# Projection of a hybrid encoder layer: four of five column groups by one level of Strassen, gate columns moved to the first group

## The reference, cut to what matters

```python
h = _rmsnorm(x, g_pre) * (1.0 + scale[:, None, :]) + shift[:, None, :]
proj = h @ w_in                       # 4096x1024 by 1024x4616, fp32
(ml_qk, ml_v, ml_o, ml_z, ml_gates,
 sb_q, sb_k, sb_v, sb_z) = jnp.split(proj, IN_SPLITS, axis=-1)
ml_qk = jax.nn.silu(_causal_conv(ml_qk, conv_w, conv_b))
i_pre = ml_gates[..., :ML_HEADS] + b_igate
f_pre = ml_gates[..., ML_HEADS:] + b_fgate
```

## Time and profile before

| what | value |
|---|---|
| median of 3 runs | 3766.06 us (3761.98 to 3766.7) |
| the profiled execution's own time | 3763.1 us |
| its span, first to last instruction | 3761.5 us |
| granted TensorE clock, mean | 0.984 |
| PE busy / DVE / ACT / POOL | 3633.8 (97%) / 2331.9 (62%) / 1841.2 (49%) / 609.4 (16%) us |
| DMA moved | 417.70 MB, mean 111 GB/s |

### The profile page before, as it was taken

How to read it: one execution, slowest core, us unless ns; L and a number is a source line. 1 busy time by engine, 2 the same in 40 slices (tenths; PEclk the granted TensorE clock), 3 DMA queues, 4 the chain that set the end, 5 groups by cost and what they waited for, 6 DMA issues and landing times. The chain is left out here.

```text
span 3761.5 us, 63114 instructions
## 1 busy us (share of the span) xinstructions
PE 3633.8 (97%) x22323; PEld 2822.3 (75%) x22323; DVE 2331.9 (62%) x3261; ACT 1841.2 (49%) x3831; POOL 609.4 (16%) x635
## 2 busy tenths in 40 slices
PE   6999999999999999997999999989999999799998
PEld 4888788878887887775777677767777777588887
DVE  3444322221216888335898899889889889466665
ACT  3333211121113223224777777777778777455554
POOL 0000033222211211000111201220001001233332
PEclk8999999999999999998999999999999999899999
DMA  7332755554333222324011201110111000466664
GB/s 241 134 134 111 269 180 180 190 200 140 131 116 107 92 94 94 131 106 151 18 31 52 72 18 41 46 63 18 35 41 57 17 11 31 147 201 200 202 202 138
DMA packets 257630, 417.70 MB, mean 111 GB/s; under 512 B 29937, under 2 KB 153201, under 8 KB 251985
## 3 DMA queue, kind: packets, MB, share of 16 engines
q1 hardware_dynamic: 248144, 389.81, 30.6%
q0 software_dynamic: 9280, 25.18, 2.4%
HBM read 272.11 MB, written 147.00 MB: 111 GB/s over the span
## 5 line engine op out<-in xcount | busy, mean ns | idle before, releaser
L1068 DVE TENSOR_TENSOR_SCAN a_prod<-a_keep,a_prod,a_zeros 128x512 f32<-128x512 f32 x896 | 1075.7, 1267 | 86.1 <-ACT a_keep L984 84.4
L993 ACT COPY a_turned<-a_rt 128x512 f32<-128x512 f32 x1088 | 546.8, 588 | 255.3 <-PE a_rt L938 255.0
L984 ACT ACTIVATE a_keep<-a_z 128x512 f32<-128x512 f32 (+3 forms) x1152 | 555.6, 573 | 43.1 <-PE a_z L927 43.0
L938 PE MATMUL a_rt<-a_ident,a_prod 128*128 128x128 f32 x4224 | 531.7, 278 | 23.2 <-DVE a_prod L1068 22.7
L938 PEld LDWEIGHTS a_rt<-a_ident,a_prod 128*128 128x128 f32 x4224 | 452.5, 141 | 132.7 <-issue 63.2
L350 PE MATMUL p_bank<-p_hhi,p_whi 128*128 128x512 f32 (+1 forms) x1344 | 526.5, 392 | 13.8 <-DVE p_wlo L631 13.7
L350 PE MATMUL p_bank<-p_hlo,p_whi 128*128 128x512 f32 (+1 forms) x1344 | 524.9, 391 | 0.0
L350 PE MATMUL p_bank<-p_hhi,p_wlo 128*128 128x512 f32 (+1 forms) x1344 | 524.6, 390 | 0.0
L949 PE MATMUL a_acc<-a_turned,a_dw 128*64 128x256 f32 x4352 | 519.8, 380 | 0.7 <-ACT a_osum L1003 0.7
L949 PEld LDWEIGHTS a_acc<-a_turned,a_dw 128*64 128x64 f32 x4352 | 286.7, 136 | 213.6 <-issue 92.5
L927 PE MATMUL a_z<-a_khi,a_q 64*128 64x512 f32 (+3 forms) x2304 | 374.1, 404 | 1.3 <-DVE a_xe L1054 0.9
(11 more groups left out here) (210 smaller groups left out, 4892.4 us busy)
## 6 DMA issues: line engine op xcount, KB each, us to landing
p_hraw<-scratch_hT SPq DMA_DIRECT2D x34, 2048.0 KB, 8.1
p_wraw<-in_x SPq DMA_DIRECT2D x8, 2048.0 KB, 8.5
scratch_hT<-p_hraw SPq DMA_DIRECT2D x8, 2048.0 KB, 6.3
m_xt<-in_x SPq DMA_DIRECT2D x32, 512.0 KB, 4.8
out_y<-m_ot SPq DMA_DIRECT2D x32, 512.0 KB, 3.7
p_wraw<-in_w_in SPq DMA_DIRECT2D x3, 4096.0 KB, 14.7
p_wada<-in_w_ada SPq DMA_DIRECT2D x16, 512.0 KB, 14.3
scratch_szg<-p_oa SPq DMA_DIRECT2D x32, 256.0 KB, 2.0
```

The source lines that it names most:

```text
L938: last = pe.transpose(rt[k % RB][:, h * QW + i * P:h * QW + (i + 1) * P], prod[:, u % PB, 2 * i + h, kb * P:(kb + 1) * P], ident[:])
L984: act.activation(keep[:, at % KB, 0:w], z[at % ZB][:, 0:w], ACT.Sigmoid, scale=-Z_SCALE).then_inc(keep_done, 1)
L993: act.copy(by_head(turned[:, k % TB]), by_head(rt[k % RB][:])).then_inc(turned_done, 1)
L1068: dve.tensor_tensor_scan(prod[:, u % PB, s, 0:w][:, ::-1], keep[:, at % KB, 0:w][:, ::-1], zeros[:, 0:w], first, ALU.mult, ALU.add).then_i ...
```

## The change

In each of the groups SPLIT, CONV, VO and GATED (now in this order) the product of a chunk is cut in two by tokens, by features and by columns, and computed with seven products of half size in place of eight (Winograd's form). For every product PE runs two banks (one in GATED) with contraction over 512 features:

- SPLIT, CONV: 2 banks x 2 halves x 12 matmuls with 256 moving columns; VO: 2 banks x 12 matmuls with 512; GATED: 1 bank x 2 halves x 12 with 256. `Seven` counts them and holds the order.
- Products 3, 5 and 6 accumulate into banks in which another product already lies; DVE's `total` adds the kept first product (ACT copies it, `kept`) to five of the seven, 2 operations each, and the results then go through the same kinds of finishing as before.
- The sums of token blocks are made once per chunk in the first group (DVE `token_sums`, 4 operations of 128x1024, stored as `sums_d`, another 2048 KB). The sums of weight blocks are made by POOL in 28 steps (`weight_sums`: two loads of 256 KB, four subtractions of 128x256, one store of 512 KB), starting when the first chunk's h and sums have been stored, and before POOL's first weight split.
- Each product's token operand is loaded (512 KB) and split in one piece of 128x1024: `high_a` on ACT, `low_a` on DVE, in CONV on POOL. There are two operand buffers (four in GATED) and three landing buffers. Weights stay for a whole group: 14 pieces of 512 KB (7 in GATED), of which the odd ones are subtracted by POOL; a piece is replaced as soon as its product of the group before is done for the last chunk.
- In CONV the first tap moves to ACT (`first_tap`), four pairs of rows are kept in `upair`, and one small copy per pair (`tail_done`) replaces two per row. POOL's differences of value rows move to VO, in 16 steps of four times the size.
- The eight gate columns leave the last group. In the first one each chunk gets a ninth block: a stationary tile that has the high gate columns at 0 to 7 and the low ones at 32 to 39, times the high tokens (8 matmuls), and the high columns times the low tokens (8 matmuls). ACT copies the second part out, DVE adds both and the bias.
- The loops over chunks in the later groups are gone; all is written out.

```diff
-            got = Count()
-            bank_free = [Count() for _ in range(8)]
-            for g, (kind, _) in enumerate(GROUPS[1:], 1):
-                with pe.Fori(0, NCH // 2) as i:
...
+            for q in range(NQ):
+                g, n, r = sv.at(q)
+                kind = sv.kinds[g]
+                if sv.low_engine(q) == "pool":
+                    pe.wait_ge(a_lop, A_LOW[q])
+                else:
+                    pe.wait_ge(a_lo, A_LOW[q])
...
+                for j in range(sv.banks(q)):
+                    bank_ready(q, j)
+                    dst = bank[ROLE[r] + j]
...
+                        for mm in range(2):
+                            f = slice((2 * j + mm) * P, (2 * j + mm + 1) * P)
+                            part = dst[:, mm * HC:(mm + 1) * HC]
+                            for k in range(4):
+                                for e, (stationary, moving) in enumerate(((wh[:, k, f], ah[:, k]), (wh[:, k, f], al[:, k]), (wl[:, k, f], ah[:, k]))):
+                                    last = pe.matmul(part, stationary, moving, ...)
```

```diff
+                    if b == 8:
...
+                        for k in range(KT):
+                            pe.matmul(dst[0:40, :], wgt[:, k], hhi[:, n % 2, k], start=k == 0, stop=False, skip_group_check=True)
+                        for k in range(KT):
+                            last = pe.matmul(dst[0:8, :], wgt[:, k, 0:8], hlo[:, n % 2, k], start=False, stop=k == KT - 1, skip_group_check=True)
```

```diff
+            def low_a(q):
+                ah, al = a_flat[a_slot(q)]
+                pool.wait_ge(a_hi, q + 1)
+                pool.tensor_tensor(al, flat(araw[q % 3]), ah.bitcast(F32), ALU.subtract).then_inc(a_lop, 1)
...
+            pool.wait_ge(n_out, 32)
+            for key in pre_count:
+                weight_sums(*key)
```

The order on ACT and DVE per step (a step is one product; both work on the product that PE has just ended):

```diff
+            for step in range(NQ + 1):
+                for q in range(step + 1, min(NQ, step + 3)):
+                    if sv.ahead(q) == step:
+                        high_a(q)
...
+                if step:
+                    finish(step - 1)
+                    taps, sigs = sv.conv_tiles(sv.TAPS, step - 1), sv.conv_tiles(sv.SIGS, step - 1)
...
+                    if q % 7 in (1, 2, 4, 5, 6):
+                        total(q)
+                    finish(q)
+                    for ci in sv.conv_tiles(sv.FIRS, q):
+                        fir(ci)
+                        if ci % 8:
+                            conv_out(ci - 1)
```

More of the change, by code:

```diff
@@ L28 @@
 C_SQ, C_SK, C_SV, C_SZ = 2568, 3080, 3592, 4104
[L31 to L51, removed]
 def identity(pool, tile, sem, n):
@@ L59, in identity @@
                        pattern=[[-1, P]], channel_multiplier=1).then_inc(sem, 1)
-CONV, SPLIT, VO, ZV, GATED = range(5)
+SPLIT, CONV, VO, ZV, GATED = range(5)
 GROUPS = [
@@ L70 @@
     (SPLIT, [(C_SQ, 1024)]),
+    (CONV, [(C_QK, 1024)]),
     (VO, [(C_V, 1024)]),
-    (CONV, [(C_QK, 1024)]),
-    (GATED, [(C_SZ, 512), (C_G, 8)]),
+    (GATED, [(C_SZ, 512)]),
 ]
@@ new lines, in a_waits, with w_width @@
+        def a_waits(q):
+            s = a_slot(q)
+            for before in range(q - 1, max(-1, q - 8), -1):
+                if a_slot(before) == s:
+                    return sv.all_done(before)
+            return sv.all_done(sv.index(sv.at(q)[0] - 1, NCH - 1, s - 2)) if s >= 2 else 0
+        def w_width(g):
+            return 2 * HC if sv.kinds[g] != GATED else HC
+        PIECE_NO, n_piece = {}, 0
+        for g in range(1, NG):
+            for m in range(7):
+                for h in range(sv.pieces(g)):
+                    PIECE_NO[g, m, h] = n_piece
+                    n_piece += 1
@@ L139, in by_ready @@
[L139 to L153, removed]
@@ L269, in _ @@
             for s in range(4):
-                sp.wait_ge(st_a[s], 16 * stored[s].now)
-                sp.wait_ge(st_b[s], 16 * stored_low[s].now)
+                sp.wait_ge(st_a[s], 16 * (1 + 2 * NCH + used_a[s]))
+                sp.wait_ge(st_b[s], 16 * (1 + used_b[s]))
+            sp.wait_ge(g_st, 16 * NCH)
         @block.tensor
         def _(pe):
-            for b in range(8):
-                pe.sem_inc(full[b], 1)
             pe.wait_ge(csil_ready, 2)
@@ L318, in _ @@
                         for q, (stationary, moving) in enumerate(hl):
[L319 removed]
+                            last = pe.matmul(dst[:], stationary, moving, start=(k == 0 and q == 0), stop=(k == KT - 1 and q == 2))
                     last.then_inc(f_full, 1)
[L321 to L323 removed]
@@ L398, in _, with quarters @@
-            pool.wait_ge(dv_out, vout.now)
+            done = [0]
+            def quarters(source, dst, first):
+                k = done[0]
+                if k:
+                    hold(pre_out, 16 * k)
+                for kh in range(2):
+                    pool.dma_start(scr[:, kh], source[:, kh]).then_inc(pre_in, 16)
+                pool.wait_ge(pre_in, 32 * (k + 1))
+                first(4 * k)
+                hold(pre_step, 4 * k + 4)
+                pool.dma_start(dst, scr).then_inc(pre_out, 16)
+                done[0] += 1
@@ L613, in _ @@
                 else:
-                    dve.wait_ge(h_hi, 1)
-                    dve.tensor_tensor(hlo[:, 0], hraw[:], hhi[:, 0].bitcast(F32), ALU.subtract).then_inc(h_lo, 1)
-                for b in range(3):
+                    low_a(0)
+                    low_w(1, 0, 0)
+                for b in range(4):
                     evict(b)
+                    if n == 0 and b == 0:
+                        token_sums(0)
                 for pair in range(PAIRS):
@@ new lines, in fir @@
+            def fir(ci):
+                n, b = ci // 8, ci % 8
+                uu, yy = upair[b // 2][:, b % 2], conv_y[ci % 4]
+                dve.wait_ge(tap_done, ci + 1)
+                for j in range(1, 4):
+                    if j > 1:
+                        dve.wait_ge(fir_step, 2 * ci + j - 1)
+                    dve.scalar_tensor_tensor(out=yy, in0=uu[:, j:j + CH], scalar=cw[:, j, b:b + 1], in1=yy,
+                                             op0=ALU.mult, op1=ALU.add).then_inc(fir_step if j < 3 else fir_done, 1)
+                if b % 2 and n + 1 < NCH:
+                    dve.wait_ge(fir_done, ci + 1)
+                    pair = upair[b // 2]
+                    dve.tensor_copy(pair[:, :, 0:3], pair[:, :, CH:CH + 3]).then_inc(tail_done, 1)
@@ new lines, in _ @@
+            for step in range(NQ + 1):
+                for q in range(step + 1, min(NQ, step + 3)):
+                    if sv.ahead(q) == step and sv.low_engine(q) == "dve":
+                        low_a(q)
+                if step:
+                    q = step - 1
+                    if q == sv.index(2, 0, 0):
+                        dve.wait_ge(n_out, 32 * NCH)
+                        dve.wait_ge(pre_out, 16 * len(pre_count))
+                        for pair in upair:
+                            dve.memset(pair[:, :, 0:3], 0.0).then_inc(tail_done, 1)
+                    if q % 7 in (1, 2, 4, 5, 6):
+                        total(q)
+                    finish(q)
+                    for ci in sv.conv_tiles(sv.FIRS, q):
+                        fir(ci)
+                        if ci % 8:
+                            conv_out(ci - 1)
+                    if q % 7 == 4 and sv.conv_chunk(q) is not None:
+                        conv_out(8 * sv.conv_chunk(q) + 7)
+                while next_w < len(W_DVE) and sv.w_step(*W_DVE[next_w][:2]) <= step:
+                    low_w(*W_DVE[next_w])
+                    next_w += 1
```

907 lines of the change are left out of this document (598 added, 309 removed).

## The result

| | kernel before | changed kernel |
|---|---|---|
| median (lowest to highest) | 3764.02 us (3760.97 to 3766.7, 4 runs) | 3730.57 us (3721.5 to 3735.73, 4 runs) |
| ratio to before | | 0.9909, 95% interval 0.9883 to 0.9934 |
| the profiled execution | 3763.1 us | 3735.73 us |
| DMA moved | 417.70 MB | 517.84 MB |

A forecast was written before the change was run, and what follows sets the result against it. PE was taken to bound the projection, DVE second in CONV. First group and start 477.4, SPLIT 317.2, CONV 357.2, VO 304.4, GATED 158.6 end it at 1614.8 instead of 1724.8; forecast 3656 us, range 3595 to 3735.

The forecast's parts named there:

- POOL ahead of the second group: Before SPLIT: 28 weight sums at 13.8 us a step end at 473.7 us, so PE waits 10 us.
- rival B: Before SPLIT: POOL late by far, 16 us a step, PE waits 72 us, total 3718 us; chance 0.12.
- the products' time: Matmuls of 256 columns in SPLIT, CONV and GATED start every 0.118 us: 6720 take 793 us.
- Rival C: Matmuls of 256 columns: weight load only half covered, pitch 0.158 us, total 3885 us, slower than before; chance 0.1.
- the sentence that the prediction takes from the Trainium skill: Matmuls: weight loads overlap only when going to another row group; full-height loads would lie behind the stream, pitch 0.21 us.
- Rival D: All products wait for operands, 0.4 us on each of 224, 90 us in all, total 3745 us; chance 0.1.
- CONV: CONV: POOL's splits block DVE's taps, 44 us a chunk against PE's 39.6; 40 us extra, 357.2 us in all.
- VO's ends: VO: 1344 matmuls at 0.2265 us, called sure at 304.4 us, with nothing added for first and last chunks.
- SPLIT's first chunk: Start of SPLIT: weight pieces follow one product ahead of PE through three landing buffers, adding 4 us (0 to 20).
- the first group: First group: gate matmuls add 29.0 us, so PE ends it at 463.4 us; DVE's token sums put at nothing.
- GATED: Last group: 1344 matmuls of 256 columns at 0.118 us, 158.6 us, operands covered.
- What follows the projection: After the projection: the last product's add, sigmoid, product and store take 2 us more than before.

The follow-up runs named there:

- the fastest version: Against the kernel with 16 sums ahead and CONV's low halves on DVE, DVE also subtracts POOL's seven VO weight pieces: 3641.31 us, ratio 0.9673.

## Why the prediction was right or wrong

**Wrong: POOL ahead of the second group.** This term of the sum carries 46 us of the 85 by which the projection ends late. The mechanism was right (PE waits for POOL's 28 sums), the price of one sum was not, and so PE's wait was put at 10 us and took 57.7. It was rival B's case at a smaller size; B stood for POOL alone, at 62 us more, and terms that B does not have bring the rest, so that 3718 lies near 3730.57 is partly chance. A step was put at 13.8 us and took (517.07 - 86.56)/28 = 15.38. The groups and waits of POOL in the first 520 us of the changed kernel say which term:

```profile
L593 POOL DMA_DIRECT2D p_u<-in_w_in x56 | 38.4, 690 | 202.1 <-DMA scratch_wsums<-p_u 119.5 <-DMA scratch_sums<-p_hraw 82.6
L608 POOL TENSOR_TENSOR p_u<-p_u 128x256 f32<-128x256 f32 x28 | 28.1, 1005 | 2.2
L602 POOL TENSOR_TENSOR p_u<-p_u 128x256 f32<-128x256 f32 x28 | 24.8, 886 | 124.1 <-DMA p_u<-in_w_in 124.1
```

Per step: the wait for the two loads 124.1/28 = 4.4 us (predicted 3.5), for the store 4.3 (4.0), load issues 38.4/28 = 1.4 (1.1), the four subtractions with what lies between 4.05 (3.8), the store's issue and what leads to it 1.3 (1.4). Each is off by under a microsecond, the wait for the loads by most (0.9); the error was to multiply means from other stretches by 28. The waits of the earlier trace rows are from SPLIT and VO of the kernel before, with one 2048 KB load per chunk; in the first group a chunk has three such transfers, and DVE has its new sums. The two stretches of before, and below them the first group of the changed kernel (columns as in the earlier trace rows):

```profile
434.40:790.00 355.60, 351.19 (x1537) 289.05 (x1536) 88.55 (x80) 73.94 (x81) 106.56 (x139) 1.00 0.56 191
790.00:1142.00 352.00, 349.19 (x1529) 287.55 (x1530) 67.29 (x49) 54.21 (x47) 78.66 (x118) 1.00 0.41 141
```

```profile
54.60:461.90 407.30, 405.58 (x1888) 325.94 (x1888) 216.46 (x281) 131.21 (x190) 138.81 (x161) 0.99 0.61 222
```

In a step of 19.5 us in which DVE made its token sums (SBUF operands, up to 1.66 us each for 1.2), POOL's subtractions take twice their time and a load is slow:

```profile
102.57 1.42 POOL L593 DMA_DIRECT2D p_u<-in_w_in  x2 [3.24 <-DMA scratch_wsums<-p_u]
111.42 1.50 POOL L602 TENSOR_TENSOR p_u<-p_u 128x256 f32<-128x256 f32 x1 [7.43 <-DMA p_u<-in_w_in]
...
116.36 1.60 POOL L608 TENSOR_TENSOR p_u<-p_u 128x256 f32<-128x256 f32 x1
118.57 0.57 POOL L597 DMA_DIRECT2D scratch_wsums<-p_u  x1 [0.61 <-POOL p_u L608]
```

and once PE, DVE and all transfers but POOL's own are idle (95 GB/s from 498 to 509 us, its 1 MB a step), a step takes 10.9:

```profile
498.20 1.07 POOL L593 DMA_DIRECT2D p_u<-in_w_in  x2 [2.95 <-DMA scratch_wsums<-p_u]
501.88 0.72 POOL L602 TENSOR_TENSOR p_u<-p_u 128x256 f32<-128x256 f32 x1 [2.62 <-DMA p_u<-in_w_in]
...
509.09 1.07 POOL L593 DMA_DIRECT2D p_u<-in_w_in  x2 [2.94 <-DMA scratch_wsums<-p_u]
```

So the company of the stretch costs a step 4.5 us on average (15.4 for 10.9). No run separates the other transfers' part of it from DVE's.

By the forecast itself POOL was already 10 us late, so 28 x 1.58 = 44 us went to the end whole, with 1.6 for the later start (86.56 for 85). The version with 16 sums ahead took the wait away, and 51 us with it.

**Right, the products' time.** Rival C, that half of the weight load lies open, fails: the pitch is 0.120 us, for 0.118. The excess over streaming read at 512 columns, 13 ns, added to 107 ns gives 0.120; that row was the better guide than the nearest one in columns. So the sentence that the prediction takes from the Trainium skill ("TensorE: Matmul & The Clock Gate", Part 3, The mechanism) does not hold here by itself: 107 ns of streaming and an uncovered load would be 0.21 us, so full-height loads of the next matmul do run beside the one in flight. The same section also lets a load into the background weight buffer be pulled ahead, which the prediction passed over; no run here shows by which way the loads go. 6720 x 0.002 = 13 us of the miss. Rival D fails as well, with PE busy for 40.30 of 40.3 us in SPLIT.

**Right, CONV.** 44.4 us a chunk for 44, and 44.3 us over 2688 x 0.120 for a predicted 40. The mechanism shows in the timelines of POOL and DVE, about the 2.38 us wait of PE in each chunk, here from 976.00 to 978.38, until the first total at 977.55:

```profile
973.67 2.62 POOL L621 TENSOR_TENSOR p_hlo<-p_wraw,p_hlo 128x1024 fp32r<-128x1024 f32 x1 [5.27 <-ACT p_hlo L708]
978.51 2.37 POOL L621 TENSOR_TENSOR p_hlo<-p_wraw,p_hlo 128x1024 fp32r<-128x1024 f32 x1 [2.23 <-ACT p_hlo L708]
```

```profile
972.51 4.33 DVE L1054 SCALAR_TENSOR_TENSOR p_ob<-p_hraw,p_cw,p_ob 128x512 f32<-128x512 f32 x3
...
976.95 0.69 DVE L1064 SCALAR_TENSOR_TENSOR p_ob<-p_ob 128x512 f32<-128x512 f32 x1
977.55 1.28 DVE L1020 TENSOR_TENSOR p_hraw<-p_wraw,p_bank 128x512 f32<-128x512 f32 x2
978.75 2.68 DVE L1064 SCALAR_TENSOR_TENSOR p_ob<-p_ob 128x512 f32<-128x512 f32 x1
```

Three taps take 4.33 us with a POOL subtraction in them (2.33 without), and the total behind them, for which PE waits, comes 2 us later. A product takes 2.68 for 0.69 and ends at 981.43, 0.55 after POOL does. A total, with PSUM as an input, keeps its 0.69 us also where it lies wholly inside a POOL subtraction (the first row is DVE's, the second POOL's):

```profile
882.20 0.69 DVE L1020 TENSOR_TENSOR p_hraw<-p_wraw,p_bank 128x512 f32<-128x512 f32 x1 [7.95 <-PE p_bank L565]
```

```profile
880.50 2.40 POOL L621 TENSOR_TENSOR p_hlo<-p_wraw,p_hlo 128x1024 fp32r<-128x1024 f32 x1 [1.76 <-ACT p_hlo L708]
```

Taking POOL out of it gave back 24.5 us of the 44.3. The remaining 20 are CONV's first chunk (45.4 - 40.3) and its last (55.1 - 40.3). One part of the term was off: 8 us were to be absorbed by PE's lead, and the first seven chunks took 309.7 us, only 1 less than 7 x 44.4. That is about CONV's 4.3 us of the miss beside the pitch.

**Partly wrong: nothing was left for VO's ends.** VO was called sure at 304.4 us and took 318.1. Its steady chunks are right (38.1); its first costs 8.4 more and its last 5.0 more. In the first, DVE still has CONV's last taps beside VO's token splits and weight pieces, and POOL's splits meet both (a token split took 3.24 us for 1.22, three taps 4.34 for 2.33). In the last, PE waits for a total that stands in DVE's order behind a token split, which waits for ACT's half of it, which waits for PE's product before (PE stands from 1528.28 us):

```profile
1528.37 1.04 ACT L708 CAST p_hlo<-p_wraw 128x1024 fp32r<-128x1024 f32 x1 [4.38 <-PE p_bank L557]
1529.45 1.23 DVE L928 TENSOR_TENSOR p_hlo<-p_wraw,p_hlo 128x1024 fp32r<-128x1024 f32 x1 [4.20 <-ACT p_hlo L708]
1530.59 1.28 DVE L1027 TENSOR_TENSOR p_y<-p_wraw,p_bank 128x512 f32<-128x512 f32 x2
1531.42 7.33 PE L557 MATMUL p_bank<-p_wlo,p_hlo 128*128 128x512 f32 x24 [3.14 <-DVE p_y L1027]
```

SPLIT's first chunk, put at 4 us over the steady one, cost 10; its last 1.4. These ends are some 21 us of the miss. In the fastest version the four chunks still take 49.0, 40.3, 42.1 and 43.1 us, so two thirds of it are left. The 3.24 us wait of before is gone, but the changes of group bring several short waits instead. PE's waits after SPLIT's start: the first two lines are CONV's (2.4 to 2.9 us in each chunk from the second on, 5.8 and 5.2 in its last), the third is of VO's first chunk, the fourth of its first and last, the fifth of SPLIT's first:

```profile
PE p_bank L565 <- DVE p_hraw L1020: 20.5, 7, 5.8
PE p_bank L565 <- POOL p_hlo L621: 9.2, 5, 5.2
PE p_bank L557 <- DVE p_hlo L928: 4.9, 2, 2.6
PE p_bank L557 <- DVE p_y L1027: 4.1, 2, 3.1
PE p_bank L565 <- POOL p_wlo L627: 3.0, 1, 3.0
```

**Right:** the first group (461.9 for 463.4) with DVE's sums at no visible cost, and GATED but for the pitch. What follows the projection took 3735.7 - 1699.7 = 2036.0 us, 2.3 less than before where 2 more was predicted.

**The sum of the miss:** 46 (POOL) + 13 (pitch) + 7.4 (SPLIT's ends) + 4.3 (CONV) + 13.7 (VO) = 84.4, less 4.3 behind the projection: 80 of the 80.7 us between 3655 and 3735.7.

**What stays open.** Why the pitch is 0.120 in some stretches and 0.113 in others with 64 stationary columns; how the 4.5 us that a step of POOL costs more in company divide between transfers and DVE; which of the waits at SPLIT's and VO's starts could be ordered away, beyond VO's weight pieces; and how much of the 14 us between the changed kernel's own runs is the varying length of POOL's steps, as only the profiled run has a trace.

## What to carry to other kernels

Work put in front of a deadline on an in-order engine is priced with the step time that it will have there, beside the transfers and neighbours of that stretch, and what is not needed for the deadline goes behind it; the gain of the whole change more than tripled (33 to 123 us) by the order of 12 sums and by which engine subtracts. But before moving it, follow each consumer through the queues: a load that stands in another engine's order asks for its source long before the multiply does. And where DVE works back to back on two SBUF inputs, it can be cheaper to give it the small job as well than to give it to idle POOL: here 1.22 us of DVE a piece cost less than 2.4 of POOL, through most of which DVE stood.

## What the runs showed of the hardware

A short stop of PE costs more than itself. PE's granted clock and busy times around the 2.38 us wait of a CONV chunk (columns as in the earlier trace rows):

```profile
976.00:978.40 2.40, 0.02 (x2) 0.05 (x1) 2.37 (x5) 1.53 (x2) 0.29 (x1) 1.00 0.00 0
978.40:980.40 2.00, 2.00 (x11) 2.00 (x12) 2.00 (x2) 0.04 (x1) 1.89 (x1) 0.57 0.89 226
980.40:982.00 1.60, 1.60 (x9) 1.60 (x9) 1.60 (x3) 0.00 (x0) 0.48 (x1) 0.50 0.62 211
982.00:984.00 2.00, 2.00 (x18) 2.00 (x18) 1.67 (x4) 1.53 (x2) 0.00 (x0) 0.97 0.77 195
```

After PE resumes, the clock is at or near its lower level, 1.2 GHz, for the 3.6 us of the second and third rows; in that time 20 matmuls start, where 30 would at 0.120. The 48 matmuls of this product took 7.47 us, those of the product before 5.92 (busy time as one row of each), so the wait of 2.38 cost 1.5 more. In the fastest version waits of 1.43 and 1.62 us were followed by products of 6.02 and 6.01 us, so nearly nothing lay behind them; one of 3.96 us was followed by 7.47. Behind the wait of 57.7 us 96 matmuls took 13.97 us, 2.4 over 96 x 0.120. DVE with seven more operations was busy for less time than without them, as "busy" counts standing: a high busy share of DVE beside a working POOL is not yet a full engine.
